# One weight piece leads for three of four tiles, and the third weight buffer goes, at three fused norm boundaries

## The reference, cut to what matters

```python
for i in range(2):
    h = x * (1.0 + scale) + shift                 # modulation, from a small product of c
    y = mixer(h)                                  # i = 0: gating and pooling; i = 1: convolution
    x = layer_norm(alpha * x + (1.0 + gate) * y, mix_ln_g[i], mix_ln_b[i])
    h = x * (1.0 + scale2) + shift2
    y = conv_ffn(h)                               # up, depthwise convolution, gelu, down
    x = layer_norm(alpha * x + (1.0 + gate2) * y, ffn_ln_g[i], ffn_ln_b[i])
```

## Time and profile before

| | |
|---|---|
| median of 3 runs | 3728.8 us (3725.64 to 3731.65) |
| the profiled execution's own time | 3725.03 us |
| its span in the profile | 3722.9 us |
| PE busy | 3230.0 us, 87% of the span |
| DVE busy | 2212.8 us, 59% |
| ACT busy | 1287.0 us, 35% |
| granted TensorE clock, mean | 0.937 of full speed |
| boundary after `ab_out`: first matmul of the last two pieces to the last DVE instruction | 194.5 to 223.1 us |
| the same after `down0` | 613.8 to 639.0 us |
| the same after `cv_out` | 894.7 to 922.7 us |

### The profile page before, as it was taken

The page is one execution under the profiler, slowest core; times in us unless marked ns, Lnnn a source line. Parts: engine busy times, 40 slices in busy tenths (PEclk is TensorE's granted clock), DMA queues, the critical chain, the costliest instruction groups (busy, mean ns, idle before and its releaser), DMA issues. The chain is left out here.

```text
span 3722.9 us, 62741 instructions
## 1 busy us (share of the span) xinstructions
PE 3230.0 (87%) x26398; PEld 2617.4 (70%) x26398; DVE 2212.8 (59%) x3950; ACT 1287.0 (35%) x2183; POOL 138.8 (4%) x178
## 2 busy tenths in 40 slices
PE   6889998976999958976776777999998899879999
PEld 5667876645887757854765766887886777658787
DVE  7678866786787465766445445554333646663344
ACT  2243334324333332144434324222233326642233
POOL 0200001100000000000101100000000000000000
PEclk9989999988999979987998988999999999989999
DMA  7535552102334212310000012322212232022231
GB/s 288 164 104 180 181 167 100 61 19 64 125 147 142 91 52 103 131 57 29 5 28 16 5 60 91 110 105 93 78 58 89 102 130 75 1 87 95 85 96 68
DMA packets 64424, 342.67 MB, mean 92 GB/s; under 512 B 15120, under 2 KB 16656, under 8 KB 28432
## 3 DMA queue, kind: packets, MB, share of 16 engines
q1 hardware_dynamic: 61904, 331.01, 25.8%
q0 software_dynamic: 2240, 7.64, 0.6%
HBM read 327.84 MB, written 10.79 MB: 91 GB/s over the span
## 5 line engine op out<-in xcount | busy, mean ns | idle before, releaser
L263 DVE TENSOR_TENSOR weight_lo<-weight_ring,weight_hi 128x1024 fp32r<-128x1024 f32 x341 | 420.5, 1235 | 152.5 <-ACT weight_hi L248 147.8
L248 ACT CAST weight_hi<-weight_ring 128x1024 fp32r<-128x1024 f32 x341 | 355.9, 1044 | 179.6 <-PE banks L420 100.7
L418 PE MATMUL banks<-hT_hi.1,weight_hi 128*128 128x512 f32 x896 | 366.4, 409 | 28.6 <-PEq L381 23.6
L419 PE MATMUL banks<-hT_lo.1,weight_hi 128*128 128x512 f32 x896 | 359.1, 401 | 0.0
L420 PE MATMUL banks<-hT_hi.1,weight_lo 128*128 128x512 f32 x896 | 358.8, 400 | 0.0
L418 PEld LDWEIGHTS banks<-hT_hi.1,weight_hi 128*128 128x128 f32 x896 | 171.5, 191 | 72.2 <-issue 26.5
L419 PEld LDWEIGHTS banks<-hT_lo.1,weight_hi 128*128 128x128 f32 x896 | 171.8, 192 | 41.5 <-issue 1.9
L420 PEld LDWEIGHTS banks<-hT_hi.1,weight_lo 128*128 128x128 f32 x896 | 171.3, 191 | 41.8
L418 PE MATMUL banks<-hT_hi.3,weight_hi 128*128 128x512 f32 (+1 forms) x512 | 175.4, 343 | 7.9 <-PEq L381 7.9
L420 PE MATMUL banks<-hT_hi.3,weight_lo 128*128 128x512 f32 (+1 forms) x512 | 174.4, 341 | 0.0
L419 PE MATMUL banks<-hT_lo.3,weight_hi 128*128 128x512 f32 (+1 forms) x512 | 174.3, 340 | 0.0
(11 more groups left out here) (742 smaller groups left out, 7768.4 us busy)
## 6 DMA issues: line engine op xcount, KB each, us to landing
weight_ring<-ff SPq DMA_DIRECT2D x64, 1024.0 KB, 4.9
weight_ring<-ada SPq DMA_DIRECT2D x48, 1024.0 KB, 4.9
weight_ring<-up SPq DMA_DIRECT2D x44, 1024.0 KB, 4.9
weight_ring<-ada_ffn SPq DMA_DIRECT2D x24, 1024.0 KB, 4.9
weight_ring<-down SPq DMA_DIRECT2D x20, 1024.0 KB, 4.9
weight_ring<-ada_mix SPq DMA_DIRECT2D x16, 1024.0 KB, 4.9
first_blocks.1<-ada_mix SPq DMA_DIRECT2D x8, 1024.0 KB, 12.0
weight_ring<-cv_in SPq DMA_DIRECT2D x8, 1024.0 KB, 4.8
```

Source lines behind the costliest of these rows:

```text
L248: self.nc.scalar.copy(hi, raw).then_inc(self.hi_made, 1)
L263: self.nc.vector.tensor_tensor(lo, raw, hi.bitcast(F32), ALU.subtract).then_inc(self.lo_made, 1)
L418: nc.tensor.matmul(out, w_hi, x_hi, start=first, stop=False)
L419: nc.tensor.matmul(out, w_hi, x_lo, start=False, stop=False)
```

## The change

The list of matrices with a third slot becomes empty, the buffer for it is no longer allocated, and in the boundary stage PE gets `lead = T - 1 = 3`: it does A for tiles 0, 1 and 2, then B for tiles 0, 1 and 2, then A and B for tile 3. With `lead` above 0, the loop takes B only when it comes to it. B takes its turn in the two slots like any other piece, and N is now in the slot of A, where it was in the slot of the piece ahead of A.

```diff
 SPREAD = ["up1", "ab_v"]
-THIRD_SLOT = ["ab_out", "down0", "cv_out"]
+THIRD_SLOT = []
@@
                 @block.tensor
                 def _(pe):
-                    token_products(pe, name, tiles, left, mm_done, evac, by_tile=2)
+                    token_products(pe, name, tiles, left, mm_done, evac, by_tile=2, lead=T - 1)
@@
         with stage():
             hT = hT_pair(SEQ)
             affine = [sb("ln_gain", [P, D]), sb("ln_bias", [P, D])]
-            weights.third_buf = [sb("third_weight_hi", [P, PIECE], F32R), sb("third_weight_lo", [P, PIECE], F32R)]
```

## The result

The changed kernel is slower: 3743.76 us against 3727.22 us (medians of 4 runs each), a ratio of 1.0043 (95% interval 1.003 to 1.0056), or +16.5 us. In a second comparison, of 8 runs with 25 of the kernel before, the ratio was 1.0037 (1.0024 to 1.005). The forecast was +17.6 us, and 3746.4 us for the time. The profiled execution took 3743.76 us itself, with a span of 3741.6.

A forecast was written before the change was run, and what follows sets the result against it. The prediction took DVE's first second-half turn to bound each boundary, with N's wait for A's slot delaying it by 4.14, 9.33 and 4.14 us: 3728.8 + 17.6 = 3746.4 us, range 3738 to 3753.

The forecast's parts named there:

- The end hangs on DVE's first turn, not on PE: At the three boundaries, the stage's end is the start of DVE's first second-half turn plus a fixed tail.
- The rival that the end of the products sets the end: PE's last product matmul sets the boundary's end: 10.0 us earlier in all, 3718.8 us; chance 4%.
- B starts 4.64 us after t: t: when PE has used up the piece ahead of A; B's casts, DVE parts and PE start follow by t + 4.64.
- The gap ahead of B is about 0.7 us: At `ab_out`, PE's gap of 3.58 us shrinks to 0.71 us, as A is done first.
- N waits for the 24th matmul after B, and DVE stands for about 3, 7 and 3 us: N's cast waits until A is used up, 5.44 us after B starts; DVE waits at `ab_out`, `down0`, `cv_out`.
- The rival that N is not held: N's cast need not wait for A, so only B's lateness stays: 4.4 us, 3733.2 us; chance 7%.
- The first turn moves by 4.14, 9.33 and 4.14: DVE's first second-half turn (line 1007) starts that many us later at `ab_out`, `down0` and `cv_out`; sum 17.6 us.
- The clock stays up: After the 0.71 us gap PE stays at 2.4 GHz; the rival of a falling clock gave 3750.9 us, chance 7%.
- Nothing makes up for it later, and other stages keep their length: Outside the three boundaries all stages keep their length; the stream cannot run ahead by more than its four blocks.
- PE idles 6 to 9 us before its first transpose: At the boundaries, after the products, PE stands idle 6 to 9 us before its first transpose.

The follow-up runs named there:

- lead 1: The kernel before with third slots kept and `lead=1`, so PE starts A before B is there; ratio 0.9985.
- the kernel with N moved as well: The kernel before with third slots kept, `lead=1`, and N's cast and low part moved later, behind the turns; ratios 0.9991 and, again, 0.9980.
- lead 0, two slots: The kernel before with the third slots given up and `lead` left at 0, PE waiting for both pieces; ratio 1.0091.

## Why the prediction was right

The medians moved by 16.5 us in the first comparison and 15.8 in the second, the boundaries by 17.3, against 17.6 forecast. The range held it, and the sign and mechanism are those of the forecast. The time itself came out 2.6 us under the 3746.4 forecast: 1.6 of that is the kernel before, whose median fell from 3728.8 with 3 runs to 3727.22 with 4. Step by step:
- *The end hangs on DVE's first turn, not on PE.* Right. PE finished 4.64 us earlier after P at `ab_out`, and the boundary became 4.05 us longer. The turns kept their 3.02 us and waited for nothing. The rival that the end of the products sets the end is out. The advice of the Trainium skill (Perfetto Trace Analysis, Optimization Strategy), to find the gaps of the engine that one optimises and make what ends them come sooner, would have called this change a gain: PE's gap went from 3.58 to 0.44 us.
- *B starts 4.64 us after t.* Measured 4.55 at `ab_out` (193.35 to 197.90). The last step was 1.27 us, from the start of B's low part to PE, where the rows of before had 1.36. This is most of the 0.1 us by which all three boundaries stayed under the sum.
- *The gap ahead of B is about 0.7 us.* The timeline has 0.44. About 0.1 is the earlier B; the rest is the way of counting. The forecast counted from where the next matmul would have started (0.233 after the last), the timeline counts from that matmul's modelled end (0.40 after its start). Counted as forecast, it is 0.61. The comparison with the 3.58 and 1.36 us of before mixed the two counts, which changes nothing in the conclusion.
- *N waits for the 24th matmul after B, and DVE stands for about 3, 7 and 3 us.* Measured 2.96, 7.17 and 2.96. The rival that N is not held is out.
- *The first turn moves by 4.14, 9.33 and 4.14.* Measured 4.06, 9.19 and 4.08.
- *The clock stays up.* Right: no matmul between B and the end of the products is at the lower level. The clock falls afterwards, in the longer idle time, and the transposes run at the lower level (8 in 1.97 us), where the first 22 of the 32 at `ab_out` ran at the upper one before (16 in 2.13 us, rows below). They have slack: from the fourth turn to the last DVE instruction it is 13.1 us, as before.
- *Nothing makes up for it later, and other stages keep their length.* Right as far as it can be seen: the rest was 3632.9 and 3630.8 us, within the scatter of the other executions, though first execution against first and second against second it is 1.5 and 2.9 us over the kernel before. Near the boundaries nothing of it shows. From the end of the first boundary to the next P it is 389.9 and 389.2 us (before: 388.9 and 389.5), from the end of the second 251.2 and 251.7 (before: 251.8 and 252.0), and the next stage's first product starts 1.65 to 1.68 us after the last DVE instruction of `ab_out` and 1.14 to 1.15 after those of the other two, in both kernels.
- *PE idles 6 to 9 us before its first transpose.* 6.56, 6.17 and 5.92: at the lower end, the last just under it.

The granted clock at `ab_out` now, over the products and in the tail, by window (PE, PEld, DVE, ACT, POOL busy, PEclk, DMA share, GB/s):

```profile
190.00:206.00 16.00, 14.72 (x62) 11.20 (x61) 11.62 (x14) 4.13 (x4) 0.00 (x0) 1.00 0.20 66
206.00:222.00 16.00, 6.68 (x28) 5.51 (x29) 12.72 (x33) 7.83 (x14) 0.00 (x0) 0.55 0.00 1
```

And the transposes at the same boundary in the kernel before, on PE's timeline:

```profile
207.33 2.13 PE L941 MATMUL banks<-identity.1,residual.1 128*128 128x128 f32 x16
211.47 0.85 PE L941 MATMUL banks<-identity.1,residual.1 128*128 128x128 f32 x6 [2.01 <-ACT residual.1 L968]
214.39 2.39 PE L941 MATMUL banks<-identity.1,residual.1 128*128 128x128 f32 x10 [2.08 <-ACT residual.1 L968]
```

## What to carry to other kernels

When a buffer is given up, ask not only when the piece that used it is late, but which piece takes the next place in the rotation, and what stands behind that one in the in-order queues. Here the piece that lost its buffer came 1.15 us later on DVE, and the prefetch behind it held up the turns of four tiles by 4 to 9 us. A prefetch belongs in a queue where its wait is already over, or where the engine waits anyway; and a gap on the busiest engine is worth nothing while another engine carries the tail.

## What the runs showed of the hardware that I had not expected

The clock did not follow the length of a gap alone. With lead 1, PE stood for 2.09 us ahead of B at `ab_out` and for 2.10 us at `cv_out`; 7 matmuls were slow (0.42 to 0.43 us from start to start) at the first and none at the second, and in the kernel with N moved as well it was the other way round, with gaps of the same length. That same kernel, executed again, had its slow matmuls at `ab_out` and none at `cv_out`. In the kernel before, by the same count, 7 were slow behind the 3.58 us at `ab_out` in one execution and 10 in the other. In "lead 0, two slots" the gap was 5.1 us from start to start at all three boundaries, and 5, 10 and 8 matmuls were slow behind it; that is most of what took its 35.6 us above the range expected. A price for the clock is therefore good to a microsecond or two at a place, not better.

The switch to the root's table cost ACT 1.28 us and nothing around it: the load starts 0.02 us after the end of the cast before it (203.85 + 1.05 to 204.92), and the first root 0.01 us after the end of the load. The Trainium skill (ScalarE: Activation LUTs, What ACT_TABLE_LOAD costs) gives 1.28 us for the load, which agrees, and a drain of 1.38 besides, of which these rows show nothing.
